# A two-layer hybrid decoder: the output projection's first two blocks in halves, and a new order of x, constants and angles

## The reference

```python
for i in range(DEPTH):                       # 2 layers
    if i % 2 == 0:
        mix = _hybrid_attention(h, positions, ...)   # layer 0
    else:
        mix = _s5_glu(h, ...)                        # layer 1: state-space scan, GELU, GLU
    h = _layernorm(ALPHA * h + mix, ln1_g[i], ln1_b[i])
    ple = (p[i] @ ple_w[i]) * sigmoid(h @ ple_gate_w[i])
    h = _layernorm(ALPHA * h + _swiglu(h, ffn_w_in[i], ffn_w_out[i]) + ple, ln2_g[i], ln2_b[i])

# _hybrid_attention
q_lat, kv_lat, k_pe, qd, kd, vd = split(h @ w_in)          # 2048 -> 512 + 512 + 64 + 3 * 1024
q  = rms(q_lat) @ w_q_b ; rotary on 64 of 192 per head      # 8 latent heads
kv = rms(kv_lat) @ w_kv_b ; k_pe rotated, shared by heads
out_a = causal attention(q, k, v)
out_b = merge of three dilated branches(qd, kd, vd)         # 8 dilated heads
return concatenate([out_a, out_b]) @ w_out                  # 2048 x 2048
```

## Time and profile before

| | |
|---|---|
| median of 3 runs | 2328.98 us (2328.63 to 2329.18) |
| profiled execution, own time | 2333.46 us |
| profiled execution, span | 2331.6 us |
| mean granted TensorE clock | 0.991 |
| TensorE busy | 2271.3 us (97%) |
| VectorE busy | 1671.6 us (72%) |
| ScalarE busy | 1033.3 us (44%) |
| DMA | 478.51 MB, mean 205 GB/s |

### The profile page before, as it was taken

How to read it: one execution, slowest core, us unless ns; L and a number is a source line. 1 busy time by engine, 2 the same in 40 slices (tenths; PEclk the granted TensorE clock), 3 DMA queues, 4 the chain that set the end, 5 groups by cost and what they waited for, 6 DMA issues and landing times.

```text
span 2331.6 us, 34852 instructions
## 1 busy us (share of the span) xinstructions
PE 2271.3 (97%) x12016; PEld 1879.8 (81%) x12016; DVE 1671.6 (72%) x2591; ACT 1033.3 (44%) x1159; POOL 216.3 (9%) x312
## 2 busy tenths in 40 slices
PE   8999999999999999999997899999999999999996
PEld 7888778888888888888787688888888888888885
DVE  5675657878888878888878656676677654677755
ACT  4545535444544334444342544544445443444432
POOL 0000048801111111000100000000000000000000
PEclk9999999999999999999998999999999999999998
DMA  6655365677887777666765366666666666666663
GB/s 231 196 183 179 99 199 173 209 247 264 269 263 253 245 243 239 220 220 222 253 244 182 116 192 194 214 224 195 201 191 187 202 192 194 194 191 189 197 197 110
DMA packets 134011, 478.51 MB, mean 205 GB/s; under 512 B 16208, under 2 KB 17840, under 8 KB 132752
## 3 DMA queue, kind: packets, MB, share of 16 engines
q1 hardware_dynamic: 119280, 427.35, 56.9%
q0 software_dynamic: 13216, 48.20, 6.5%
q10 hardware_dynamic: 1408, 1.51, 0.2%
HBM read 457.85 MB, written 19.14 MB: 205 GB/s over the span
## 4 chain that ended last, share of the span: by engine, by line
PE 91%; DVE 5%; DMA 1%; issue 1%; ACT 1%; POOL 0%; SPq 0%; DVEq 0%; ACTq 0%
PE ps L373 29%; PE ps L374 29%; PE ps L375 29%; PE ps L695 1%; DMA s_bt_raw<-in_s_bt 1%; PE ps L720 1%; DMA raw<-in_w_in 1%; DVE w_lo L1106 1%; DVE scan_work L1799 1%; PE ps L404 0%; DVE gated L1435 0%; PE ps L515 0%; DVE scan_work L1803 0%; DVE chain L1805 0%; PE ps L531 0%
## 5 line engine op out<-in xcount | busy, mean ns | idle before, releaser
L1106 DVE TENSOR_TENSOR w_lo<-raw,w_hi 128x1024 fp32r<-128x1024 f32 x775 | 949.3, 1230 | 533.9 <-ACT w_hi L773 525.5
L773 ACT ACTIVATE w_hi<-raw 128x1024 fp32r<-128x1024 f32 x775 | 817.9, 1059 | 990.1 <-PE ps L375 863.0
L373 PE MATMUL ps<-w_hi,x_hi 128*128 128x512 f32 x2304 | 902.2, 392 | 7.9 <-DVE w_lo L1106 4.9
L375 PE MATMUL ps<-w_hi,x_lo 128*128 128x512 f32 x2304 | 898.5, 390 | 0.0
L374 PE MATMUL ps<-w_lo,x_hi 128*128 128x512 f32 x2304 | 898.4, 390 | 0.0
L373 PEld LDWEIGHTS ps<-w_hi,x_hi 128*128 128x128 f32 x2304 | 433.7, 188 | 99.1 <-issue 5.0
L375 PEld LDWEIGHTS ps<-w_hi,x_lo 128*128 128x128 f32 x2304 | 433.6, 188 | 91.1
L374 PEld LDWEIGHTS ps<-w_lo,x_hi 128*128 128x128 f32 x2304 | 433.7, 188 | 88.7
L373 PE MATMUL ps<-w_hi,hid_hi 128*128 128x512 f32 x704 | 275.7, 392 | 1.8 <-DVE w_lo L1106 1.8
L374 PE MATMUL ps<-w_lo,hid_hi 128*128 128x512 f32 x704 | 274.2, 389 | 0.0
L375 PE MATMUL ps<-w_hi,hid_lo 128*128 128x512 f32 x704 | 274.0, 389 | 0.0
(11 more groups left out here) (250 smaller groups left out, 1326.8 us busy)
## 6 DMA issues: line engine op xcount, KB each, us to landing
raw<-in_w_inA SPq DMA_DIRECT2D x192, 512.0 KB, 4.3
raw<-in_w_inB SPq DMA_DIRECT2D x160, 512.0 KB, 4.2
raw<-in_w_outA SPq DMA_DIRECT2D x96, 512.0 KB, 3.5
raw<-in_w_outB SPq DMA_DIRECT2D x80, 512.0 KB, 4.3
raw<-in_w_in SPq DMA_DIRECT2D x64, 512.0 KB, 4.4
raw<-in_w_gate SPq DMA_DIRECT2D x64, 512.0 KB, 4.2
raw<-in_w_glu SPq DMA_DIRECT2D x64, 512.0 KB, 4.3
raw<-in_w_out SPq DMA_DIRECT2D x32, 512.0 KB, 4.1
```

The lines of the kernel that those rows point to most:

```text
L373: pe.matmul(o, hi[:, kt + k, cols], WH[:, s, k, 0:width], start=(kt + k == 0), stop=False)
L375: last = pe.matmul(o, lo[:, kt + k, cols], WH[:, s, k, 0:width], start=False, stop=(kt + k == depth - 1))
L773: act.activation(WH[:, s, :, 0:width], RAW[:, s, :, 0:width], ACT.Copy).then_inc(hi_ready, 1)
L1106: dve.tensor_tensor(WL[:, s, :, 0:width], RAW[:, s, :, 0:width], WH[:, s, :, 0:width].bitcast(F32), ALU.subtract).then_inc(lo_ready, 1)
```

## The change

It has two parts.

Start. x comes in eight transfers of 256 KB, one before the first weight chunk, one after each of the first four, the other three behind them. TensorE turns x one step ahead instead of two: `turn_x(0)` and `turn_x(1)` before chunk 0, then `turn_x(j + 1)` before chunk j. ScalarE issues only the identity; GpSimd issues p, gains, positions, frequencies and ln1 rows once three high halves are made, the mask and the first biases once eight are. p is turned before chunk 10 instead of chunk 6, the ln1 rows in block 2 instead of block 1, and the angles are computed in three parts behind the low halves of chunks 17, 18 and 19.

Output projection. The first two blocks run by halves: chunks 0 to 3 of block 0, chunks 0 to 3 of block 1, chunks 4 to 7 of block 0, chunks 4 to 7 of block 1. `wout_place(n)` gives block and chunk of the n-th. Steps 10 to 17 of the attention follow the first eight, one each. Both accumulators are open at once. SP loads the same chunks in the new order, the first sixteen written out. ScalarE casts one more chunk in each of steps 16, 17 and 18 (before, none there). VectorE takes block 0 out after the low half of the 16th chunk and block 1 after that of the 21st.

```diff
-        x_in = [sem(f"x_in{n}") for n in range(4)]
+        x_in = [sem(f"x_in{n}") for n in range(8)]
...
+        def wout_place(n):
+
+            return (n // 8, n % 8) if n >= 2 * 8 else (n // 4 % 2, n % 4 + 4 * (n // 8))
...
-            def load_x(q4):
-                cols = slice(WB * q4, WB * (q4 + 1))
-                sp.dma_start(RES[:, :, cols], xv[:, :, cols]).then_inc(x_in[q4], 16)
+            def load_x(g):
+                cols = slice(256 * g, 256 * (g + 1))
+                sp.dma_start(RES[:, :, cols], xv[:, :, cols]).then_inc(x_in[g], 16)
 
             load_x(0)
-            load_x(1)
...
                     for j in range(first):
                         load(w, j, j, 0, None, width)
-                        if j < 2:
-                            load_x(2 + j)
+                        load_x(1 + j)
+                    for g in range(first + 1, 8):
+                        load_x(g)
...
-            phase("wout", "w_out")
+            for n in range(2 * 8):
+                b, j = wout_place(n)
+                load(t["w_out"], 8 * b + j, PHASES["wout"][2] + n, 0, None, WB)
+            phase("wout", "w_out", first=2 * 8)
...
             def turn_x(g):
-                if g % 2 == 0:
-                    pe.wait_ge(x_in[g // 2], 16)
+                pe.wait_ge(x_in[g], 16)
...
                     if b == 0:
-                        if j < 6:
-                            turn_x(j + 2)
-                        elif j == 6:
-                            pe.wait_ge(p_in, 16)
-                            turn(TG["p0"], PK[:], 0)
+                        if 1 <= j < 7:
+                            turn_x(j + 1)
                         pe.wait_ge(turned, TG["x"] + j + 1)
-                    if b == 1 and j == 0:
+                    if b == 1 and j == 2:
+                        pe.wait_ge(p_in, 16)
+                        turn(TG["p0"], PK[:], 0)
+                    if b == 2 and j == 0:
                         pe.wait_ge(const_in, 10 * 16)
...
-            def mix_chunk(j):
+            def mix_chunk(n):
 
+                b, j = wout_place(n)
                 if j == 0:
-                    acc_ready(b0)
+                    acc_ready(b0 + b)
                 pe.wait_ge(mix_ready, 2 * j + 2)
-                chunk(c0 + j, 0, None, XH, XL, 2 * j, KT, b0 % 2)
+                chunk(c0 + n, 0, None, XH, XL, 2 * j, KT, (b0 + b) % 2)
...
-            for j, steps in enumerate([(10,), (11,), (12,), (13,), (14,), (15, 16), (17,), ()]):
-                mix_chunk(j)
-                for s in steps:
-                    attention_step(s)
-            for b in range(1, 4):
+            for n in range(2 * 8):
+                mix_chunk(n)
+                if n < 8:
+                    attention_step(n + 10)
+            for b in range(2, 4):
...
         def _(act):
             act.dma_start(ID[:], t["ident"]).then_inc(ident_in, 16)
-            for dst, name in [(CM[:], "causal"), (PI[:], "pos")]:
-                act.dma_start(dst, t[name]).then_inc(const_in, 16)
...
-            act.dma_start(PK[:], t["p"][0].rearrange("(t p) n -> p t n", p=P)).then_inc(p_in, 16)
...
-                    if b == 0 and j == 7:
+                    if b == 1 and j == 4:
                         hi_turned(TG["p0"], PH[:])
...
                 if s < 2 * HEADS:
                     exps(s)
-                    hi(QB[2] + 7 + s)
-            for c in range(c0 + 9, c0 + 32):
+                hi(QB[2] + 7 + s)
+            for c in range(c0 + 12, c0 + 32):
                 hi(c)
...
-                    if j == 0 and b == 1:
-                        angles()
+                    if b == 2 and 1 <= j <= 3:
+                        angles(j - 1)
...
             def wout_end(b):
-                end("wout", b)
+                dve.wait_ge(w_used, PHASES["wout"][2] + (12, 16, 24, 32)[b])
...
-            for b in range(4):
-                for j in range(8):
-                    if 8 * b + j >= 10:
-                        lo(c0 + 8 * b + j)
-                    if b and j == 4:
-                        wout_end(b - 1)
+            for n in range(10, 32):
+                lo(c0 + n)
+                if n in (15, 20, 28):
+                    wout_end((15, 20, 28).index(n))
...
+            pool.wait_ge(hi_ready, 3)
+            pool.dma_start(PK[:], t["p"][0].rearrange("(t p) n -> p t n", p=P)).then_inc(p_in, 16)
+            pool.dma_start(NG[:], t["norm_gain"].partition_broadcast(P)).then_inc(const_in, 16)
+            pool.dma_start(PI[:], t["pos"]).then_inc(const_in, 16)
+            for q in range(TT):
+                pool.dma_start(AT[:, 3, q, :], t["inv_freq"].partition_broadcast(P)).then_inc(const_in, 16)
+            for n_ in range(2 * LAYERS):
+                src = t[("ln1_g", "ln1_b")[n_ % 2]][n_ // 2:n_ // 2 + 1, :].rearrange("a (k p) -> (a k) p", p=P)
+                pool.dma_start(G1R[KT * n_:KT * (n_ + 1)], src).then_inc(const_in, 16)
+            pool.wait_ge(hi_ready, 8)
+            pool.dma_start(CM[:], t["causal"]).then_inc(const_in, 16)
+            pool.dma_start(B0[:], t["dil_bias"][:, 0:2]).then_inc(const_in, 16)
             pool.wait_ge(w_used, PHASES["qb"][2])
```

More of the change, by code:

```diff
@@ L1132, in rsqrt, with angles @@
                     link(dve.scalar_tensor_tensor(y, tmp, 1.5, y, ALU.add, ALU.mult))
-            def angles():
-                dve.wait_ge(const_in, 10 * 16)
-                dve.wait_ge(ln1_turned, 1)
-                dve.tensor_copy(G1[:].rearrange("p l c k -> p (l c k)"), Y[:, 0, 0:2 * LAYERS * KT]).then_inc(ln1_cols, 1)
+            def angles(part):
                 two_pi = 2 * np.pi
@@ L1143, in angles @@
                 c4 = float(np.float32(two_pi - c1 - c2 - c3))
-                link(dve.tensor_copy(SC[:, 8:10], PI[:]))
-                for q in range(TT):
-                    link(dve.tensor_scalar(AT[:, 0, q], AT[:, 3, q], SC[:, 8 + q:9 + q], None, ALU.mult))
                 r, n_ = AT[:, 0], AT[:, 1]
-                link(dve.tensor_scalar(n_, r, 1.0 / two_pi, ROUND, ALU.mult, ALU.add))
-                link(dve.tensor_scalar(n_, n_, -ROUND, None, ALU.add))
-                for c in (c1, c2, c3, c4):
-                    link(dve.scalar_tensor_tensor(r, n_, -c, r, ALU.mult, ALU.add))
-                dve.tensor_scalar(r, r, float(np.float32(3.1415925)), -float(np.float32(3.1415925)), ALU.min,
-                                  ALU.max).then_inc(trig, 1)
+                if part == 0:
+                    dve.wait_ge(const_in, 10 * 16)
+                    dve.wait_ge(ln1_turned, 1)
+                    dve.tensor_copy(G1[:].rearrange("p l c k -> p (l c k)"), Y[:, 0, 0:2 * LAYERS * KT]).then_inc(ln1_cols, 1)
+                    link(dve.tensor_copy(SC[:, 8:10], PI[:]))
+                    for q in range(TT):
+                        link(dve.tensor_scalar(AT[:, 0, q], AT[:, 3, q], SC[:, 8 + q:9 + q], None, ALU.mult))
+                    link(dve.tensor_scalar(n_, r, 1.0 / two_pi, ROUND, ALU.mult, ALU.add))
+                elif part == 1:
+                    link(dve.tensor_scalar(n_, n_, -ROUND, None, ALU.add))
+                    for c in (c1, c2):
+                        link(dve.scalar_tensor_tensor(r, n_, -c, r, ALU.mult, ALU.add))
+                else:
+                    for c in (c3, c4):
+                        link(dve.scalar_tensor_tensor(r, n_, -c, r, ALU.mult, ALU.add))
+                    dve.tensor_scalar(r, r, float(np.float32(3.1415925)), -float(np.float32(3.1415925)), ALU.min,
+                                      ALU.max).then_inc(trig, 1)
             def cosine():
```

8 lines of the change are left out of this document (1 added, 7 removed).

## The result

The changed kernel takes 2319.43 us (median of 5, 2316.5 to 2320.42). The kernel before, run beside it, takes 2329.18 (median of 5, 2328.63 to 2331.81). The ratio is 0.9949, with a 95% interval of 0.9938 to 0.9959: 11.9 us of 2329.2, between 9.6 and 14.4. The medians themselves are 9.8 us apart. The forecast was 2317.8, range 2314.5 to 2322.0.

What follows compares the result with a forecast made beforehand. TensorE, busy 97% of the span, was taken as the bound, so only its idle or slow time counts. Start −4.9 and projection −6.3 sum to −11.2 us, from a median of 2328.98 to 2317.8 us, range 2314.5 to 2322.

Steps and rivals of the forecast that it cites:

- First chunk: Start: early table load and no weight wait move the first chunk from 12.38 to 10.3 us, −2.1 us.
- Chunks 1 and 2: Start: the steps to chunks 1 and 2 shrink from 4.32 and 4.92 to 3.20 us each, −2.8 us.
- One step of lead: Block 0: turning x one step ahead costs +0.5 us, 0.4 of it at chunk 7; +2 with restarts.
- rival 1: Start gives only half, through restarts in the one-step chain and small x rows or late constants; 2321 us, chance 0.15.
- p, the ln1 rows and the angles: Blocks 1 and 2: three-part angles remove a TensorE wait, −0.9 us; p's transpose now stands between chunks, +0.35 us.
- Constants: Start: constants issued from GpSimd's queue land within about 11.5 us of issue and cost 0; other end +2 us.
- Rival 3: Slower: constants from GpSimd's queue land late and hold ScalarE; 2336 us at a 30 us landing, chance 0.03.
- Start together: Sum of the start's terms up to the attention: −4.9 us, between −6 and −2.5.
- Projection: End of attention: new chunk order removes waits of 1.7 and 3.0 us and 1.6 of half clock, −6.3 us.
- rival 2: Projection gives part: half clock comes anyway or step 16 still waits; total −8 to −9.6, 2320 to 2321 us, chance 0.10.
- Rival 4: No change: S5 layer "issue" waits pay the gain back, three more of 4 us giving 2329 us, chance 0.04.
- Block 1's accumulator, the emptying of block 0, GpSimd's tables: Projection and after: accumulator already free, block 0 emptied with 7 us to lose, tables begin earlier; no added wait.

Runs made afterwards that it cites:

- const_on_act: Changed kernel with constants and p issued by ScalarE at the start again; first chunk at 11.78 us, shift behind block 2 −3.62 us against −4.51.
- const_pool_at_once: Changed kernel without GpSimd's two waits, so p and the constants are issued from the start; first chunk at 14.20 us, shift −1.09 us.
- start_only: Kernel before with the start part of the change alone, output projection order as before; ratio 0.9982 (0.9973 to 0.9992).
- hi_late: Changed kernel with ScalarE's casts of chunks 9 to 11 behind the attention's steps again; projection gained 6.48 us instead of 6.78.
- angles_whole: Changed kernel with the angles in one piece behind chunk 17's low half; shift behind block 2 −4.58 us against −4.51.
- fill_split: Changed kernel with filling matmuls placed 2, x0's transposes, 6, x1's transposes, 1; 2320.76 us, ratio 0.9956 (0.9942 to 0.9970).
- angles_whole_early: Changed kernel with the angles in one piece behind chunk 16's low half; shift went from −4.46 to −3.04 us across block 2.
- Steps_paired: Changed kernel with attention steps 15 and 16 side by side again, new chunk order kept; projection gained 4.89 us instead of 6.78.
- Before_again: Kernel before, unchanged, profiled once more; shift +0.61 us up to the projection, −1.00 behind it, with the chunk behind the pause at full clock, 2.76 us.
- turns_first: Changed kernel without the six filling matmuls ahead of the transposes; 2322.14 us, ratio 0.9955 (0.9940 to 0.9971).

## Why the prediction was right, point by point

The forecast of −11.2 us stands against 11.9 (9.6 to 14.4) by the ratio. In the traces 11.3 us of the 13.0 lie at the places of the change, and 1.7 in the rest behind the first S5 transposes, which is inside what that stretch does by itself. That 11.3 meets 11.2 so closely is partly luck: the start gave 0.4 less and the projection 0.5 more, and 1.6 of the 11.3 hang on a fall of the clock that a second profile of the kernel before does not have (point 7). The time of 2319.43 is 1.6 us above the forecast of 2317.8, which took a saving seen in one execution, 4.48 us above the median, off the median; the traces can't say whether that is the reason.

1. **First chunk: −2.1 expected, −1.4 measured.** Table load at once and w_hi without a wait came true; that the table load mattered did not (const_on_act has it late and its first chunk does not wait for it). The end of 10.3 was missed since the identity landed 0.6 us later and TensorE's own queue moved with it. The working left the identity where it was. It landed at 3.47 to 3.62 us in the three profiles with the old start and at 3.94 to 4.33 in nine profiles with the new order of x, so the delay seems to go with the new order; const_pool_at_once (3.57) speaks against it, and no run isolates the reason. That queue and w_lo came out nearly level, as the working had it (10.29 and 10.3, measured about 11 and 10.83). In start_only, the same start, it was 10.73. What set the time was TensorE's filling and no longer the data (in hi_late and angles_whole, where the filling took 2.40 us, there was a short wait of 0.18 and 0.32 us again); fill_split showed that 1.9 us more were to be had.
2. **Chunks 1 and 2: −2.8 expected, −2.84 measured.** From 10.98 to 17.38 is 6.40 us, against 9.24 before. x in eight transfers cost nothing that TensorE felt.
3. **One step of lead: +0.5 expected, +0.39 measured.** From chunk 2 to chunk 7 it is 16.05 us instead of 15.66, with four turns between them in both. It falls at chunk 7, where the working put 0.4: the trace shows 0.20 of it as idle (the row at 33.43), the rest as a matmul drawn longer than the pitch to the next. The steps before stay at 3.20 to 3.24 us, so the chain shows no restart cost, and rival 1 is out.
4. **p, the ln1 rows and the angles: −0.9 + 0.35 expected, −1.17 measured.** From chunk 7 to chunk 10 it is 8.64 us instead of 9.81. With p's turn at +0.35 and the ln1 rows' at −0.29, which comes back in block 2, the angles' wait is worth about 1.2. Of the 5.0 us that stand at chunk 10, 0.5 are given back by block 2: 0.1 behind p's turn, 0.4 at the ln1 rows' turn. The step that was argued wrongly is the split. The sum held that VectorE needs the angles in pieces to stay under its idle time; angles_whole lost nothing. The wait comes when the angles follow the low half right behind the turn, as angles_whole_early shows.
5. **Constants: 0 expected, 0 measured.** They landed in 2.7 to 6.0 us, and no wait of ScalarE for them shows. ScalarE did wait 4.00 and 0.50 us for weights just behind the last of them (until 38.86 and 40.42 us), which TensorE did not feel; hi_late, with the same transfers, has no such wait over 0.2, so they are not shown to be its cause. The Trainium skill (SBUF — State Buffer, section "SBUF: two separate sides") speaks of VectorE locking GpSimd out of writing descriptors; this trace shows no such delay in these transfers, which were issued amid VectorE's low halves. Whether VectorE was in the mode that the page means while they were issued, no run shows, so the rule is not put to the test here. Rival 3 did not happen. What GpSimd's transfers did in const_pool_at_once is another thing: issued at the start, they came with x and w late there.
6. **Start together: −4.9 expected, −4.5 measured** (−4.69 in start_only). The first chunk alone is 0.7 short, and the other terms together give 0.3 more than expected. Block 0 was done 4.0 us earlier (chunk 8), where the working had about 4.5.
7. **Projection: −6.3 expected, −6.78 measured.** 1.72 and 3.01 are the waits, 1.62 the half clock (4.37 against the 2.75 to 2.76 of a chunk at full clock), and 0.43 is left, which I put down to the hand-overs, the upper bound of 6.6 being 0.2 short. Steps_paired shows 0.17 of it beside the wait for probs; the rest no run isolates. Before_again says that the 1.6 counts only in executions in which the clock fell. Against one like it the projection gives 5.2. So rival 2's case for the clock is partly right: the 1.6 is a gain of some executions, not of all, and the forecast should have counted it at less than whole. (Rival 2's −8 to −9.6 gives 2321.0 to 2319.4; the working wrote 2320 for the low end. Rival 4's three waits of 4 us give 2329.8, not 2329.)
8. **Block 1's accumulator, the emptying of block 0, GpSimd's tables: hidden, as expected.** From chunk 8 to the first S5 transposes it is 907.5 us in both traces. (In the other profiles it is up to 1.2 us more or less, so the exact match is chance.)
9. **Rival 4, S5's "issue" waits paying it back: did not happen as a rule.** They went from 7.7 us to 6.6, and lie between 4.6 (hi_late) and 8.1 us (fill_split) in the 14 profiles. In fill_split's profile they did eat the gain: 1.6 us ahead at the S5 layer, and 1.7 us more in the rest.

The variation of the rest can be placed further than its total says. It all arises in the first 215 us behind the first S5 transposes; from there to the end the profiles agree within 0.1 us. And it goes with the clock: in the 70 us that begin 60 us behind those transposes the granted clock is 0.95 in eight profiles, with rests of 1110.1 to 1112.8 us, and 0.98 in the other six, with 1107.8 to 1110.2. In the two profiles of the kernel before the windows are:

```profile
1278.80:1348.80 70.00, 59.26 (x1382) 48.59 (x1375) 48.70 (x119) 36.90 (x46) 0.73 (x1) 0.95 0.37 119
...
1276.70:1346.70 70.00, 60.72 (x1398) 50.04 (x1391) 49.93 (x120) 37.84 (x47) 0.73 (x1) 0.98 0.37 124
```

What stays open is why the clock falls there, and after the pause of the projection, in some executions and not in others, and what makes the rest of the variation.

## What to carry to other kernels

When one engine is the bound, add up its waits by place and check each later against the same matmul's start in the new trace, before and behind the place of the edit; that finds a gain of 1 us where the rest of the span varies by 5. Profile the unchanged kernel twice before you count a slow clock as something to be won. Where two instructions of a pipeline stand side by side, put independent work between them. Hold transfers that nobody wants yet behind a semaphore of the work instead of only moving them to another queue, and after each gain at the start look at which queue ends last, for it may be the filling.

## What the runs showed that was not expected

- The same constants, issued at the start, cost TensorE some 0.5 to 0.9 us from ScalarE's queue and 3.4 from GpSimd's. The second 256 features of x were there at 10.03 us instead of by about 7.9. VectorE had no instruction before 8.0 us in that trace, so its work was not the reason.
- The 20 filling matmuls took 2.40 to 3.15 us in the ten profiles without a pause over 0.52 us before them, and 4.39 or 4.02 behind one of 1.73 or 2.68 us. The window behind the second pause reads a granted clock of 0.63, the one behind the first 1.00, so the clock's row does not tell of every slow matmul at the start:

```profile
8.50:10.50 2.00, 2.00 (x11) 2.00 (x11) 1.57 (x3) 1.54 (x2) 0.00 (x0) 1.00 1.05 406
```

(turns_first, its window 8.5 to 10.5 us: eleven matmuls where the changed kernel has eighteen.)

- One and the same pause of 3.01 us was followed by half clock in two profiles and by full clock in a third.
- A stretch of some 1110 us that no edit touches took between 1107.8 and 1112.8 us in 14 profiles, the longer ones with the lower granted clock in the S5 layer.
- TensorE's first matmuls start 0.21 us apart, the later ones 0.11. In the ten profiles above the step lies between 7.0 and 10.3 us, and where it lies moves the first chunk: two profiles alike in TensorE's rows up to 8.64 us stood 0.6 us apart behind block 2.
